# The next layer's norm moved into the last down product of a two-layer transformer block

## The chip, the cores and the metric

The kernel runs on one core of a Trainium2 chip. The metric is the device time of one execution in microseconds, inputs in HBM at the start and the output in HBM at the end. Engines: PE (TensorE) multiplies and transposes, ACT (ScalarE) squares, rounds and evicts, DVE (VectorE) does two-operand work, POOL (GpSimd) takes inverse roots and does part of the two-operand work, SP (SyncE) issues the DMAs.

## What is computed

Two layers of a block with 1024 tokens and model width 1024, all in float32:

```
for layer in range(2):
    h = rms_norm(x) * attn_norm[layer]
    d_q, d_k, d_v, m_cq, m_ckv, m_krope, r_q, r_k, r_v, r_g = split(h @ w_in[layer])
    mixed = concat(diff_attention(...), mla(...), retention(...))
    x = x + mixed @ w_out[layer]
    h = rms_norm(x) * ffn_norm[layer]
    x = x + (silu(h @ w_gate[layer]) * (h @ w_up[layer])) @ w_down[layer]
out = rms_norm(x) * final_norm
```

## The kernel before

Each float32 operand of a product is split into a high part that the fast matmul form holds exactly (ACT rounds it by a copy) and a low part, the difference (DVE or POOL subtracts). A product is three matmuls: high by high, high by low, low by high.

Every engine has its own program, and semaphores order them; there is no scheduler. The layer is a hardware loop on each engine (`with pe.Fori(0, DEPTH) as L` and its likes), so each wait on a count of `L * PER[name] + n` takes register instructions.

The 1024 tokens are 8 tiles of 128. `X` holds x as rows. The start of a layer is the norm: ACT squares the tiles in the order 4, 5, 6, 7, 0, 1, 2, 3 (`square_rows`), POOL takes the inverse roots of four tiles at a time (`inverse_roots`), DVE scales the four tiles into `rows` or `rows1` (`scale_rows`). PE then transposes each group of four tiles in 8 blocks of 4 transpositions (`transpose_rows`), one block to a PSUM bank, four banks in turn (`NORM_BANKS`). From a bank ACT writes the high part `ht_hi` (`high_rows`) and DVE the low part `ht_lo` (`low_rows`), and then the bank is free (`tr_free`). Tiles 4 to 7 go first, then 0 to 3; all 16 blocks come before the first projection. The weights of the first head (`w_diff` 0) are rounded by ACT in four quarters and their low parts are made by POOL (`weights(0)`).

Then comes differential attention, steps `a` from -8 to 33. Up to step -1 a step projects one tile (`diff_project`, unit `u = a + 8`, tile `7 - u`, 24 matmuls of 384 columns); from step -7 on the previous unit's q and k are transposed behind it (`diff_transpose`, 4 transpositions, banks 5 and 6 in turn, `TR_BANKS`, which `take_ring` hands out). ACT takes v from the projection (`diff_v`, tile `dv`), DVE and POOL rotate q and k, ACT and DVE write them into tiles that lie over `X`; so `X` is first stored to HBM (`x_saved`), and ACT waits for that.

The layer ends with the down product, 77 steps (`DN_STEPS`) of 12 matmuls of 512 columns, seven groups of 11. ACT and DVE prepare the operands of a step four to five steps ahead (`down_high`, `down_low`), and `take_down` adds a finished group's banks to `X`. Group 4, the sixth, completes tiles 4 to 7 of `X`. Group 3, the seventh, completes tiles 0 to 3 and uses banks 0 to 3; banks 4 to 7 are not written in it. SP's queue issues the load of the next operands, one DMA a step, then in the next pass of the loop eight small loads of parameters, the three loads of head 0's weights, the three of head 1's after the last down step, and the store of `X`.

## Time and profile before

| | |
|---|---|
| Time, median of 3 runs | 2698.19 us (2694.29 to 2698.67) |
| The profiled execution's own time | 2699.12 us |
| Its span, first to last instruction | 2697.2 us |
| Mean granted TensorE clock | 0.981 |
| PE busy | 2549.1 us, 95% of the span |
| DVE, ACT, POOL busy | 1532.3, 1095.3, 1015.7 us |
| Where the first layer's last matmul starts | 1344.07 us |

The rows further down are from this one execution. Its time is 1.9 us above its span and 0.93 us above the median. In a timeline row the first number is the start, the second the time from there to the end of the group, then engine, line, instruction, output and inputs, shape, and the count; in brackets stands how long the engine was idle before it and which instruction ended that.

### The profile page before, as it was taken

The numbers are of one execution on the slowest core, as the hardware profiler recorded it, in microseconds if no ns is written. First come the engines' busy times: TensorE is split into PE (matmuls) and PEld (weight loads), VectorE is DVE, ScalarE is ACT, GpSimd is POOL, SyncE is SP. The second block draws the span as 40 slices with busy tenths as digits, with TensorE's granted clock in tenths as the row PEclk, the third lists the DMA queues.
The fourth block names the chain that finished last, engine by engine and source line by source line (L and its number), as shares of the span: only waits on it lengthen the run. The fifth ranks groups of instructions, "written<-read, shape, count | busy, mean of one in ns | idle before, by whom it ended". The sixth has DMA issues, their size and how long they took to land. (4 is left out here: it accounts for less than half of the span.)

```text
span 2697.2 us, 43066 instructions
## 1 busy us (share of the span) xinstructions
PE 2549.1 (95%) x13054; PEld 2186.6 (81%) x13054; DVE 1532.3 (57%) x3045; ACT 1095.3 (41%) x2503; POOL 1015.7 (38%) x1161
## 2 busy tenths in 40 slices
PE   5999988999899999999989999989998999999997
PEld 5999877878688888888789998777786888888886
DVE  4666555382655454577656665444726544444885
ACT  4444554262522232344444545433625322232444
POOL 3455422173254545201044554221833454542012
PEclk9999999999999999999999999989999999999999
DMA  5111011023233333573321101011232333236633
GB/s 178 28 34 39 16 37 38 4 88 134 77 106 98 96 110 108 187 254 98 106 99 32 35 20 40 5 38 42 80 123 63 111 109 109 82 113 228 217 98 121
DMA packets 238651, 242.68 MB, mean 90 GB/s; under 512 B 27904, under 2 KB 171008, under 8 KB 238464
## 3 DMA queue, kind: packets, MB, share of 16 engines
q1 hardware_dynamic: 238464, 240.43, 27.8%
q8 instruction: 88, 1.44, 0.2%
q14 instruction: 99, 0.81, 0.1%
HBM read 172.75 MB, written 67.63 MB: 89 GB/s over the span
## 5 line engine op out<-in xcount | busy, mean ns | idle before, releaser
L2414 POOL TENSOR_TENSOR fw_a_lo<-fw_a_raw,fw_a_hi 128x512 fp32r<-128x512 f32 x132 | 179.7, 1362 | 468.0 <-DVE fw_s_raw L1996 468.0
L2414 POOL TENSOR_TENSOR fw_s_lo<-fw_s_raw,fw_s_hi 128x512 fp32r<-128x512 f32 x176 | 229.7, 1318 | 51.7 <-ACT fw_s_hi L1487 51.7
L723 PE MATMUL banks<-ht_hi,da_hi 128*128 128x512 f32 x496 | 192.9, 389 | 0.0
L723 PE MATMUL banks<-ht_lo,da_hi 128*128 128x512 f32 x496 | 192.9, 389 | 0.0
L723 PE MATMUL banks<-ht_hi,da_lo 128*128 128x512 f32 x496 | 192.9, 389 | 0.0
L723 PE MATMUL banks<-w_diff_hi,ht_hi 128*128 128x384 f32 x512 | 180.7, 353 | 6.3 <-DVE ht_lo L1674 4.3
L723 PE MATMUL banks<-w_diff_hi,ht_lo 128*128 128x384 f32 x512 | 172.8, 337 | 0.0
L723 PE MATMUL banks<-w_diff_lo,ht_hi 128*128 128x384 f32 x512 | 172.6, 337 | 0.0
L2241 POOL TENSOR_TENSOR qk_rot<-rope_a,rope_b 128x512 f32<-128x512 f32 x64 | 82.7, 1292 | 210.7 <-DVE rope_b L1703 210.7
L1731 DVE TENSOR_REDUCE stats<-banks 128x1 f32<-128x1024 f32 (+3 forms) x192 | 138.3, 748 | 32.8 <-PE banks L924 27.9
L723 PE MATMUL banks<-h_t_hi,fw_s_hi 128*128 128x512 f32 x352 | 139.8, 397 | 12.1 <-DVE h_t_lo L2000 8.2
L1561 ACT ACTIVATE u_two<-u_two 128x512 f32<-128x512 f32 x42 | 26.6, 632 | 284.0 <-DVE u_two L2107 284.0
L723 PE MATMUL banks<-h_t_hi,fw_s_lo 128*128 128x512 f32 x352 | 139.2, 395 | 0.0
L723 PE MATMUL banks<-h_t_lo,fw_s_hi 128*128 128x512 f32 x352 | 139.1, 395 | 0.0
L723 PE MATMUL banks<-ht_hi,fw_a_hi 128*128 128x512 f32 x352 | 137.4, 390 | 0.9 <-POOL fw_a_lo L2414 0.9
L723 PE MATMUL banks<-ht_hi,fw_s_hi 128*128 128x512 f32 x352 | 137.0, 389 | 0.0
L723 PE MATMUL banks<-ht_hi,fw_a_lo 128*128 128x512 f32 x352 | 137.0, 389 | 0.0
L723 PE MATMUL banks<-ht_hi,fw_s_lo 128*128 128x512 f32 x352 | 137.0, 389 | 0.0
L723 PE MATMUL banks<-ht_lo,fw_a_hi 128*128 128x512 f32 x352 | 137.0, 389 | 0.0
L723 PE MATMUL banks<-ht_lo,fw_s_hi 128*128 128x512 f32 x352 | 136.9, 389 | 0.0
L2064 DVE TENSOR_TENSOR da_lo<-da_raw,da_hi 128x512 fp32r<-128x512 f32 x154 | 117.1, 760 | 23.0 <-ACT da_hi L1538 23.0
L1299 ACT ACTIVATE pt_hi<-banks 128x512 fp32r<-128x512 f32 (+1 forms) x96 | 43.7, 490 | 205.1 <-PE banks L826 205.1
(357 smaller groups left out, 7497.7 us busy)
## 6 DMA issues: line engine op xcount, KB each, us to landing
da_raw<-act_scratch SPq DMA_DIRECT2D x154, 256.0 KB, 2.7
fw_a_raw<-in_w_gate_dram SPq DMA_DIRECT2D x88, 256.0 KB, 3.1
act_scratch<-act_s SPq DMA_DIRECT2D x66, 256.0 KB, 2.9
w_diff_raw<-in_w_in_dram SPq DMA_DIRECT2D x24, 512.0 KB, 6.0
fw_a<-in_w_up_dram SPq DMA_DIRECT2D x44, 256.0 KB, 3.2
fw_a_raw<-in_w_up_dram SPq DMA_DIRECT2D x44, 256.0 KB, 2.9
act_scratch<-act_zero SPq DMA_DIRECT2D x44, 256.0 KB, 2.4
act_scratch<-act_one SPq DMA_DIRECT2D x44, 256.0 KB, 2.8
```

Of the source, the lines that this page charges most:

```text
L723: mm = pe.matmul(bank, lhsT, rhs, start=first and i == 0, stop=last and i == len(pairs) - 1, skip_group_check=resumes)
L1299: act.activation(hi[:, b:b + n, :], banks[:, TR_BANKS[r % 2], 0:n * P].rearrange("p (b n) -> p b n", n=P), ACT.Copy).then_inc(S["tr_hi"], 1)
L1561: act.activation(u2[1 - m][:], u2[1 - m][:], ACT.Silu).then_inc(S["u_g1"], 1)
L1731: dve.tensor_reduce(neg_max[:, a % 2, m:m + 1], SCORE[j % 2][:, 0:(t + 1) * P], AX_X, ALU.max, negate=True)\
L2064: dve.tensor_tensor(a[1][:], a[2][:], a[0][:].bitcast(F32), ALU.subtract)
L2241: return pool.tensor_tensor(dst[:] if copies > 1 else dst[:].unsqueeze(2), a, b, ALU.add)
L2414: pool.tensor_tensor(w[1][:], w[2][:], w[0][:].bitcast(F32), ALU.subtract).then_inc(S["f_lo"], 1)
```

## The change

The layer loop becomes a Python loop on every engine, so the program of a layer is written out twice, and waits compare with constants. Within it three pieces move.

First, the norm of tiles 4 to 7 of the next layer (squares on ACT, `square_first`; scaling on DVE, `scale_first`; 32 transpositions on PE, `first_half`; high and low parts, `high_first`, `low_first`) is issued inside or right behind the last steps of the down product: the squares behind ACT's operands of the last four steps, the transpositions ahead of PE's last two steps. For the first layer they stand ahead of the layers.

Second, the 32 transpositions of tiles 0 to 3 (`second_half`) move behind the second and the third projection, 16 each, and use banks 5 and 6 of `take_ring` instead of four banks. In the second layer DVE scales those tiles at step -7, ahead of its rotation of the second unit.

Third, the low parts of head 0's weights go from POOL to DVE (`weights_first`, semaphore `w_lo0`); at the layer boundary DVE does them, ahead of `scale_first`. ACT rounds these weights behind its last square at the boundary, and behind the first half's high parts in the first layer. The store of `X` is split in two; the half with tiles 4 to 7 is issued ahead of head 1's loads. The exponentials of lambda move from the layer's start to step -4. The table load that ACT has before its first squares is gone from its program; one stands at step -4 of each layer instead, ahead of those exponentials.

```diff
+SECOND_HALF = {1 - T: range(KD // 2), 2 - T: range(KD // 2, KD)}
+SQUARE_STEP, TRANSPOSE_STEP = 4, 2
...
-            with sp.Fori(0, DEPTH) as L:
+            for L in range(DEPTH):
...
+                def save_x(half, done):
+                    tiles = slice(4 * half, 4 * half + 4)
+                    sp.wait_ge(S[f"x_in{half}"], 16)
+                    sp.wait_ge(S["x_done"], L * PER["x_done"] + done)
+                    arrives(x_dram.rearrange("(t p) d -> p t d", p=P)[:, tiles, :], X[:, tiles, :], f"x_saved{half}")
+
+                save_x(1, T // 2)
...
                 sp.wait_ge(S["d_step"], L * PER["d_step"] + STEP_CREDIT)
                 load_diff(1)
-
-                sp.wait_ge(S["x_in0"], 16)
-                sp.wait_ge(S["x_in1"], 16)
-                sp.wait_ge(S["x_done"], L * PER["x_done"] + X_CREDIT)
-                arrives(x_dram.rearrange("(t p) d -> p t d", p=P), X[:], "x_saved")
+                save_x(0, T)
 
...
+            def first_half(layer):
+
+                pe.wait_ge(S["n_xn"], layer * PER["n_xn"] + T // 2)
+                for k in range(KD):
+                    if k >= 4:
+                        pe.wait_ge(S["tr_free"], layer * PER["tr_free"] + k - 3)
+                    for j in range(4):
+                        tr = pe.transpose(banks[:, NORM_BANKS[k % 4], tokens(j)], rows[:, j, tokens(k)], ident[:])
+                    tr.then_inc(S["tr_done"], 1)
+
+            first_half(0)
+            for L in range(DEPTH):
+                ring, freed = [KD], [0]
 
...
-                transpose_rows(rows, "n_xn", 4)
-                transpose_rows(rows1, "n_xn", 8)
                 ring_empty()
 
+                def second_half(blocks):
+                    pe.wait_ge(S["n_xn"], L * PER["n_xn"] + T)
+                    for k in blocks:
+                        bank = take_ring()
+                        for j in range(4):
+                            tr = pe.transpose(bank[:, tokens(j)], rows1[:, j, tokens(k)], ident[:])
+                        tr.then_inc(S["tr_done"], 1)
 
...
+                    if a in SECOND_HALF:
+                        second_half(SECOND_HALF[a])
...
+                    if i == DN_STEPS - TRANSPOSE_STEP and L + 1 < DEPTH:
+                        first_half(L + 1)
...
+            def square_first(layer, i):
+
+                t = NORM_TILES[i]
+                if t % 4 == 0:
+                    act.wait_ge(S[f"x_in{t // 4}"], 16)
+                act.wait_ge(S["x_done"], layer * PER["x_done"] + i + 1)
+                if i:
+                    act.wait_ge(S["n_sq"], layer * PER["n_sq"] + i)
+                act.activation(row_square[:], X[:, t, :], ACT.Square, accum_out=row_ss[:, t:t + 1]).then_inc(S["n_sq"], 1)
+
+            def high_first(layer):
+                act.wait_ge(S["params_in"], layer * PER["params_in"] + PER["params_in"])
+                for k in range(KD):
+                    act.wait_ge(S["tr_done"], layer * PER["tr_done"] + k + 1)
+                    act.activation(ht_hi[:, k, tokens(4, 4)], banks[:, NORM_BANKS[k % 4], :], ACT.Copy,
+                                   scale=attn_gain[:, k:k + 1]).then_inc(S["tr_hi"], 1)
+
+            def weights_first(layer):
+                act.wait_ge(S["w_in0"], layer * PER["w_in0"] + 16 * 3)
+                for i in range(PARTS):
+                    k = slice(i * KD // PARTS, (i + 1) * KD // PARTS)
+                    act.activation(w_diff[0][0][:, k, :], w_diff[0][2][:, k, :], ACT.Copy).then_inc(S["w_hi"], 1)
+
+            for i in range(T):
+                square_first(0, i)
+            high_first(0)
+            weights_first(0)
+            for L in range(DEPTH):
+                ring = [KD]
...
-                for i, t in enumerate(NORM_TILES):
-                    if t % 4 == 0:
-                        act.wait_ge(S[f"x_in{t // 4}"], 16)
-                    square_rows(0, i, t, "x_done", i + 1)
-                act.wait_ge(S["params_in"], L * PER["params_in"] + PER["params_in"])
-                high_rows(1, attn_gain)
-                weights(0)
-                high_rows(0, attn_gain)
-
-                act.wait_ge(S["lam"], L * PER["lam"] + 2)
-                act.activation(lam_exp[:], lam_sum[:], ACT.Exp).then_inc(S["lam"], 1)
-
+                if L:
...
+                    if a in SECOND_HALF:
+                        high_second(SECOND_HALF[a])
+                    if a == 1 - T:
+                        act.wait_ge(S["x_saved0"], L * PER["x_saved0"] + 16)
...
+                    if L + 1 < DEPTH and i >= DN_STEPS - SQUARE_STEP:
+                        square_first(L + 1, i - DN_STEPS + SQUARE_STEP)
                     if i == PAIRS + B_RING - 1:
                         act.wait_ge(S["d_step"], L * PER["d_step"] + (PAIRS + STEP_CREDIT))
                         for j in range(4):
                             act.activation(d_s1[:, j, :], banks[:, j, :], ACT.Copy).then_inc(S["d_s1"], 1)
+                if L + 1 < DEPTH:
+                    weights_first(L + 1)
+                    act.wait_ge(S["db_lo"], L * PER["db_lo"] + PER["db_lo"])
+                    high_first(L + 1)
...
+            def weights_first(layer):
+                for i in range(PARTS):
+                    k = slice(i * KD // PARTS, (i + 1) * KD // PARTS)
+                    dve.wait_ge(S["w_hi"], layer * PER["w_hi"] + i + 1)
+                    w = dve.tensor_tensor(w_diff[0][1][:, k, :], w_diff[0][2][:, k, :], w_diff[0][0][:, k, :].bitcast(F32), ALU.subtract)
+                w.then_inc(S["w_lo0"], 1)
+
+            dve.wait_ge(S["params_in"], PER["params_in"])
+            scale_first(0, 1)
+            low_first(0, range(4))
+            scale_first(0, 0)
+            low_first(0, range(4, KD))
+            weights_first(0)
+            for L in range(DEPTH):
...
-                dve.wait_ge(S["params_in"], L * PER["params_in"] + PER["params_in"])
-                scale_rows(range(4, T), 1, (rows1, rows))
-
-                low_rows(1, attn_gain, range(4))
-                scale_rows(range(4), 2, (rows1, rows))
-                low_rows(1, attn_gain, range(4, KD))
-                low_rows(0, attn_gain)
-
                 for m in range(2):
...
+                    if L and a == 1 - T:
+                        scale_first(L, 0)
+                    if a == 5 - T:
+                        lambdas()
...
+                    if a in SECOND_HALF:
+                        low_second(SECOND_HALF[a])
...
+                if L + 1 < DEPTH:
+                    weights_first(L + 1)
+                    dve.wait_ge(S["params_in"], (L + 2) * PER["params_in"])
+                    scale_first(L + 1, 1)
+                    low_first(L + 1, range(KD))
                 take_down(3)
...
                 inverse_roots(0, [(4, T), (0, 4)], 0)
-                weights(0)
```

PE at the start of a layer, before: the last rows of the transpositions (`rows_225` is `rows1`, tiles 0 to 3) and what stands between them and the first projection (L723).

```order
L750 REGISTER_ALU
L744 REGISTER_ALU [waits n_xn]
L754 MATMUL banks<-ident,rows_225 128x128 [waits tr_free]
L754 MATMUL banks<-ident,rows_225 128x128 x3
...
L737 REGISTER_ALU
L760 ISA [waits tr_free]
L761 ISA [waits w_hi]
L723 MATMUL banks<-w_diff_hi,ht_hi 128x384 [waits w_lo]
L723 MATMUL banks<-w_diff_lo,ht_hi 128x384
```

PE in the first layer of the change, from the end of the second projection (L730) to the start of the third; `qk_rot_153` is the first unit's q and k.

```order
L730 MATMUL banks<-w_diff_hi,ht_lo 128x384
L804 MATMUL banks<-ident,rows_225 128x128 [waits n_xn]
L804 MATMUL banks<-ident,rows_225 128x128 x7
L804 MATMUL banks<-ident,rows_225 128x128 [waits tr_free]
L804 MATMUL banks<-ident,rows_225 128x128 x3
...
L819 MATMUL banks<-ident,qk_rot_153 128x128 [waits tr_free,rope_sum]
L819 MATMUL banks<-ident,qk_rot_153 128x128 x3
L730 MATMUL banks<-w_diff_hi,ht_hi 128x384 [waits z_free,w_lo0,w_hi]
```

The transpositions of tiles 0 to 3 no longer stand ahead of all projections, but behind two of them, and the third waits behind four blocks of them and the first unit's four transpositions.

PE in the change, in the last group of the first layer's down product: the last matmul of step 74, the transpositions of tiles 4 to 7 for the next layer, the first matmuls of step 75.

```order
L730 MATMUL banks<-db_hi_276,da_lo_268 128x512
L745 MATMUL banks<-ident,rows 128x128 [waits n_xn]
L745 MATMUL banks<-ident,rows 128x128 x15
L745 MATMUL banks<-ident,rows 128x128 [waits tr_free]
L745 MATMUL banks<-ident,rows 128x128 x3
...
L730 MATMUL banks<-ht_hi,da_hi_270 128x512 [waits db_lo]
L730 MATMUL banks<-ht_lo,da_hi_270 128x512
```

Steps 75 and 76 of the down product now stand behind a wait for `n_xn`, the count of tiles that DVE has scaled.

ACT at the layer boundary, before: the last operands of the down product (`da_hi`, then the other operand's high part) and the end of the hardware loop; the squares follow in the next pass.

```order
L1538 ACTIVATE da_hi_273<-da_raw_275 128x512 [waits da_in6]
L1551 REGISTER_ALU [waits wd22c]
L1553 ACTIVATE ht_hi<-wd_tail 128x512 [waits d_step]
L1211 REGISTER_ALU
L1211 COMPARE_AND_BRANCH
```

ACT there in the change: the last operands, the fourth square, the weights of head 0 (`w_diff_hi`), the high parts of tiles 4 to 7, the squares of tiles 0 to 3, and the first projection's v.

```order
L1599 ACTIVATE da_hi_273<-da_raw_275 128x512 [waits da_in6]
L1614 ACTIVATE ht_hi<-wd_tail 128x512 [waits d_step,wd22c]
L1249 ACTIVATE row_square,stats<-X 128x1024 [waits n_sq,x_done]
L1262 ACTIVATE w_diff_hi<-w_diff_raw 128x768 [waits w_in0]
L1262 ACTIVATE w_diff_hi<-w_diff_raw 128x768 x3
L1255 ACTIVATE ht_hi<-banks,stats 128x512 [waits tr_done,params_in,db_lo]
L1255 ACTIVATE ht_hi<-banks,stats 128x512 [waits tr_done] x7
L1249 ACTIVATE row_square,stats<-X 128x1024 [waits n_sq,x_done,x_in0]
L1249 ACTIVATE row_square,stats<-X 128x1024 [waits n_sq,x_done] x3
L1331 ACTIVATE dv_124<-banks 128x128 [waits z_done,x_saved1]
```

The high parts of tiles 4 to 7 and the weights have moved from behind all eight squares to behind four of them.

## Rows read from the trace of the kernel before

**Rows 1.** The page, engines: busy us (share of span) x instructions.
```profile
PE 2549.1 (95%) x13054; PEld 2186.6 (81%) x13054; DVE 1532.3 (57%) x3045; ACT 1095.3 (41%) x2503; POOL 1015.7 (38%) x1161
```

**Rows 2.** Waits of PE, whole span: us in total, times, longest.
```profile
PE banks L754 <- DVE rows L1662: 30.2, 4, 22.3
```

**Rows 3.** Timeline of PE, layer boundary: start, duration, instruction, count, idle before.
```profile
1344.07 0.39 PE L723 MATMUL banks<-ht_hi,da_lo 128*128 128x512 f32 x1
...
1351.89 5.70 PE L754 MATMUL banks<-ident,rows 128*128 128x128 f32 x32 [7.43 <-DVE rows L1662]
...
1360.25 5.82 PE L754 MATMUL banks<-ident,rows 128*128 128x128 f32 x32 [2.65 <-DVE ht_lo L1674]
...
1368.24 0.46 PE L723 MATMUL banks<-w_diff_hi,ht_hi 128*128 128x384 f32 x1 [2.18 <-DVE ht_lo L1674]
```

**Rows 4.** Timeline of ACT, second layer: a dv row starts when a projection ends.
```profile
1374.27 0.28 ACT L1277 ACTIVATE dv<-banks 128x128 fp32r<-128x128 f32 x1 [5.64 <-PE banks L723]
...
1378.43 0.28 ACT L1277 ACTIVATE dv<-banks 128x128 fp32r<-128x128 f32 x1 [3.88 <-PE banks L723]
...
1383.06 0.28 ACT L1277 ACTIVATE dv<-banks 128x128 fp32r<-128x128 f32 x1 [3.53 <-PE banks L723]
...
1387.66 0.28 ACT L1277 ACTIVATE dv<-banks 128x128 fp32r<-128x128 f32 x1 [3.51 <-PE banks L723]
```

**Rows 5.** Timeline of DVE, layer boundary.
```profile
1344.50 2.48 DVE L2172 TENSOR_TENSOR X<-X,banks 128x512 f32<-128x512 f32 x4 [12.24 <-PE banks L723]
...
1356.80 2.73 DVE L1662 TENSOR_SCALAR rows<-X,stats 128x1024 f32<-128x1024 f32 x4
...
1359.45 8.54 DVE L1674 SCALAR_TENSOR_TENSOR ht_lo<-banks,stats,ht_hi 128x512 fp32r<-128x512 f32 x12
```

**Rows 6.** Timeline of ACT, layer boundary.
```profile
1330.90 0.63 ACT L1553 ACTIVATE ht_hi<-wd_tail 128x512 fp32r<-128x512 f32 x1 [1.57 <-PE banks L723]
...
1345.30 1.06 ACT L1230 ACTIVATE row_square<-X 128x1024 f32<-128x1024 f32 x1 [5.37 <-DVE X L2172]
```

**Rows 7.** Timeline of POOL, layer boundary: the second root.
```profile
1350.64 1.40 POOL L2199 TENSOR_TENSOR stats<-stats 128x4 f32<-128x4 f32 x1
```

**Rows 8.** Timeline of SP's queue, layer boundary.
```profile
1290.09 35.69 SPq L516 DMA_DIRECT2D da_raw<-act_scratch  x14
...
1329.30 0.39 SPq L516 DMA_DIRECT2D stats<-in_attn_norm_dram  x1
...
1333.59 14.01 SPq L516 DMA_DIRECT2D w_diff_raw<-in_w_in_dram  x6
```

**Rows 9.** DMA issues at 1333 to 1344: KB each, us to landing.
```profile
w_diff_raw<-in_w_in_dram SPq DMA_DIRECT2D x3, 512.0 KB, 7.2
```

**Rows 10.** DMA issues at 1344 to 1350: KB each, us to landing.
```profile
x_scratch<-X SPq DMA_DIRECT2D x1, 4096.0 KB, 15.5
```

**Rows 11.** Timeline of all engines, first layer's start.
```profile
11.89 1.28 ACT L1230 ACT_TABLE_LOAD   x1
...
22.30 6.02 PE L754 MATMUL banks<-ident,rows 128*128 128x128 f32 x32 [22.30 <-DVE rows L1662]
...
29.22 3.05 ACT L1224 ACTIVATE w_diff_hi<-w_diff_raw 128x768 fp32r<-128x768 f32 x4
...
30.05 8.43 DVE L1674 SCALAR_TENSOR_TENSOR ht_lo<-banks,stats,ht_hi 128x512 fp32r<-128x512 f32 x12
...
38.70 0.43 PE L723 MATMUL banks<-w_diff_hi,ht_hi 128*128 128x384 f32 x1 [2.15 <-DVE ht_lo L1674]
```

**Rows 12.** Timeline of ACT, first layer: the fourth projection's end.
```profile
56.54 0.28 ACT L1277 ACTIVATE dv<-banks 128x128 fp32r<-128x128 f32 x1 [3.51 <-PE banks L723]
```

**Rows 13.** Windows: length, busy of PE, PEld, DVE, ACT, POOL, then granted clock.
```profile
80.00:88.00 8.00, 6.30 (x33) 5.37 (x33) 5.96 (x10) 2.61 (x5) 1.27 (x1) 1.00 0.28 67
...
1412.00:1420.00 8.00, 6.30 (x25) 5.39 (x24) 6.66 (x10) 2.34 (x4) 1.27 (x1) 0.79 0.16 38
...
1368.00:1372.00 4.00, 3.76 (x13) 3.76 (x14) 0.87 (x7) 0.20 (x1) 0.00 (x0) 0.57 0.02 6
```

More of the change, by code:

```diff
@@ L87 @@
 DIFF_STEPS = range(-T, DIFF_HEADS * T + 2)
+SECOND_HALF = {1 - T: range(KD // 2), 2 - T: range(KD // 2, KD)}
+SQUARE_STEP, TRANSPOSE_STEP = 4, 2
 def diff_rings():
-    ring, after = 2 * KD, {}
+    ring, after = KD, {}
     for a in DIFF_STEPS:
+        ring += len(SECOND_HALF.get(a, ()))
         if 0 <= a - 1 < DIFF_HEADS * T:
@@ L1647, in _, with scale_first, low_first @@
             dve.wait_ge(S["tab_act"], 1)
-            with dve.Fori(0, DEPTH) as L:
-                ring, high = [0], [0]
+            def scale_first(layer, half):
+                dve.wait_ge(S["n_rstd"], layer * PER["n_rstd"] + (1 if half else 2))
+                for j in range(4):
+                    t = 4 * half + j
+                    dve.tensor_scalar((rows if half else rows1)[:, j, :], X[:, t, :], row_rstd[:, t:t + 1], None, ALU.mult)\
+                        .then_inc(S["n_xn"], 1)
+            def low_first(layer, blocks):
+                for k in blocks:
+                    dve.wait_ge(S["tr_hi"], layer * PER["tr_hi"] + k + 1)
+                    at_ = tokens(4, 4)
+                    dve.scalar_tensor_tensor(ht_lo[:, k, at_], banks[:, NORM_BANKS[k % 4], :], attn_gain[:, k:k + 1],
+                                             ht_hi[:, k, at_].bitcast(F32), ALU.mult, ALU.subtract).then_inc(S["tr_free"], 1)
+            def weights_first(layer):
[11 more added lines that the diff above has]
+            for L in range(DEPTH):
+                ring, high = [KD], [KD]
                 def low_ring():
@@ L2199, in inverse_root @@
                 return pool.tensor_tensor(out_, in_, minus_half[:, 0:in_.shape[1]], ALU.pow)
-            with pool.Fori(0, DEPTH) as L:
+            for L in range(DEPTH):
                 def inverse_roots(norm, groups, done):
```

52 lines of the change are left out of this document (34 added, 18 removed).

## Prediction

> **What bounds the kernel now.** I read the page first: PE is busy for 95% of the span [rows 1], so a microsecond counts only if it adds or removes idle time of PE, work of PE, or a stretch at its lower clock. PE's waits put the norm's share at 30.2 us in four places, of which 22.3 us are the time before the first transposition of all [rows 2]. Then I read PE's timeline at the boundary between the layers. The last matmul of the down product starts at 1344.07, and the first projection at 1368.24. Between lie 7.43 us of waiting for squares, root and scaling, 5.70 us of transpositions, 2.65 us of waiting, 5.82 us of transpositions, 2.18 us of waiting [rows 3]. That projection then ends at 1374.27 and the next one 4.16 us later [rows 4]; the first took 6.0 us, since the granted clock was 0.57 in its first 4 us [rows 13], the lower of the two levels (1.2 GHz) for most of it: about 1.7 us lost. The fourth projection, my mark in both layers, ends at 1387.66 in the second layer [rows 4] and at 56.54 in the first [rows 12].
>
> **What a moved transposition costs.** Before, 32 transpositions take 5.7 to 5.8 us with four banks, partly at the low clock [rows 3]; PE stands idle around them anyway. In the change the 32 of tiles 0 to 3 come behind the second and third projection, where PE has no idle time: successive projection ends are 4.16 us apart without transpositions, 4.63 and 4.60 with four (1378.43, 1383.06, 1387.66) [rows 4], so four transpositions cost 0.46 us of a busy PE. A piece of 16 costs 1.85 us if nothing waits. But they have two banks now. A bank comes free when ACT has copied it (0.69 us, my estimate; a copy of 128x512 between SBUF tiles takes 0.63 [rows 6]) and DVE has subtracted (8.54 us for 12 gives 0.71 us each [rows 5]). From a projection's end I count: block 0 and 1 written at 0.5 and 1.0; ACT on block 0 to 1.2, DVE to 1.95; block 2 written at 2.65 (with 0.2 us of signal and drain), ACT to 3.35, DVE to 4.1; then the q and k transpositions, which take block 2's bank, to 4.75. Without the change they would end at 0.46. So a piece adds 4.3 us, the two pieces 8.6 us a layer. The bound below is 3.7 us a layer (no waits), the bound above 8.6 plus clock losses.
>
> **First layer.** The first squares lose the table load ahead of them, 1.28 us [rows 11]; I count it in full. PE's first transpositions (22.30, 6.02 us long) are thus at 21.0 to 27.0. DVE's low parts start the second time at 30.05, twelve in 8.43 us, 0.70 apart [rows 11]; only four remain ahead of the weights, to 32.9, less 1.28 is 31.6. The weights' low parts are new on DVE: four of 128x768. The nearest rows are four two-operand adds of 128x512 in 2.48 us [rows 5], 0.62 each; times 1.5 is 0.93, with overlap 3.6 us for four (bounds 3.4 and 3.8). ACT has rounded the first quarter long before (29.22 plus 0.8, less 1.28 [rows 11]). First projection: 35.3, against 38.70 before [rows 11]. PE has then been idle for 8 us, longer than the 7.43 us after which the boundary shows the low clock, so I give it the 6.0 us of the second layer's first projection: ends 41.3, then 45.5. Then piece (4.75), projection (4.16), piece, projection: 63.3. Before: 56.54. **The first layer loses 6.8 us.**
>
> **The boundary.** A down step takes 2.72 us: 14 loads, one a step, in 35.69 us [rows 8]. Step 75, of 0 to 76, would start at 1344.46 less 5.44, at 1339.0. PE waits there until DVE has scaled tiles 4 to 7, and DVE does the weights first. The squares fit: ACT stands idle 1.57 us in a step [rows 6] and a square takes 1.06 [rows 6] plus a short readout; they end at about 1333. The weights decide. SP's last operand load is issued by 1325.78, the small loads begin only at 1329.30 and the weights' at 1333.59 [rows 8]; the 3.5 us between are the end of the loop, as nothing is waited for. Unrolled, the weights' load starts at 1330.1. Before, the third lands some 7.7 us after the first issue (7.2 us median from issue [rows 9]); so they are there at 1337.8. ACT's first quarter takes 0.8, DVE 3.6, scaling 2.73 [rows 5]: PE goes on at 1345.1, **6.1 us late**. Queued behind it are two steps of the down product, and behind these `take_down(3)`, the last squares and all that follows. The transpositions take 5.7 us as they did before [rows 3] (four banks, the same copies behind them), the two steps 5.44: the product ends at 1356.2, against 1344.46. High and low parts of tiles 4 to 7 are finished by then and hidden. Two projections at the full clock end at 1364.6. Meanwhile `take_down(3)`, squares and root follow the product's end as before: the root ends at 1350.64 plus 1.40, 7.6 us after it [rows 7], here 1363.8; scaling to 1366.5. PE waits 1.9 us once more. Piece, projection, piece, projection: 1384.4, against 1387.66. **The boundary gains 3.3 us.**
>
> SP: the second half of the store is issued behind head 1's loads. The whole store of 4 MB took 15.5 us from issue [rows 10]; half of it, issued at about 1359.5 behind 1.5 MB, lands around 1369 to 1370 by my estimate. ACT waits for it ahead of the first q and k at about 1371, so it costs nothing, with 1 to 2 us of cover; each further microsecond of delay would hold the third projection. POOL only loses work. ACT's new table load at step -4 is hidden: it is idle for 3.5 us in a projection step [rows 4].
>
> **Registers.** Counting the programs' rows, a layer of PE loses some 700 register instructions, ACT and DVE as many. Where an engine is busy they lie behind its work. They can only lengthen a wait that is passed while another stands behind it. The view of waits has some 100 waits of PE in the whole span; at 0.015 us each (a choice near the 0.04 us of a whole hop, below) that is 1.5 us. The bounds are 0 and 10 us (0.1 each).
>
> **Sum.** Plus 6.8, minus 3.3, minus 1.5 is plus 2.0 us. The pieces leave PE idle for some 2 of 5 us, four times. Two stretches of 8 us, one in each layer and both with 6.30 us of PE work, differ: one has clock 1.00, the other 0.79 [rows 13]. At 1.7 us a fall I add one of four: plus 3.7 us on 2699.12. The profiled execution is 0.93 us above the median, so against the median's kind of run: **2702 us**. A difference under 0.2%, 5.4 us, is about what cannot be told from none.
>
> **Rivals.**
> - *Forecast: the pieces on two banks eat what the boundary gives.* 2702, own range 2697 to 2708. Chance 0.45.
> - *Faster: the register instructions count on every hop.* In latency-bound stretches a result passes ACT, DVE and POOL before PE gets it. If each of the 100 waits of PE is 0.1 us shorter, 10 us go: 2693. It decides above 0.12 us a wait, given the plus of 5 us from the rest. For it: there are many such instructions. Against: the one hop that the rows show, from PE's last matmul (ends 1344.46) to DVE's add at 1344.50 [rows 3, 5], takes 0.04 us with registers in the program. Chance 0.16.
> - *The clock falls in each piece.* Four falls instead of one: plus 5 us, 2707; with a fall in the last down steps too, 2709. For it: the second stretch of [rows 13]. Against: the first one, with the same idle time. Chance 0.19.
> - *The weights land later at the boundary,* since the store of tiles 4 to 7 (2 MB) is issued right behind them and shares the DMA engines, or SP gains nothing from the unrolled loop: 3.5 us later, 2705.5; with the store's other half late too, 2709. Chance 0.12.
> - *PE does not wait at step 75,* because the weights are early: 6 us less, 2696. Against: [rows 8, 9] would have to be off by 6 us. Chance 0.08.
>
> The Trainium skill, page "TensorE: Matmul & The Clock Gate", section "A second HAM failure mode: psum-queue depth-cycling", describes a kernel that cycles through PSUM banks, idles briefly between groups of matmuls, and so loses and regains its clock again and again. By that rule the third case would hold, 2707 instead of 2702. The trace has it both ways [rows 13], and I keep to one fall.
>
> **How the numbers follow.** Slower by over 0.2% (above 2703.6): a third of the forecast's 0.45, nearly all of the clock's 0.19, most of the late weights' 0.12: 0.42. Faster (below 2692.8): half of the register case and tails of the others: 0.14. Within: 0.44. The range, 2692 to 2710, leaves out the far half of the register case and the worst of the clock and weights cases.
>
> **What would show it.** In the changed kernel: first projection at 35 in the first layer, fourth ending near 63; a wait of PE for `rows` of 6 us near 1352 (all is 7 us later there) inside the down product; 1.9 us more before the second layer's first piece; ACT and DVE alternating in each piece with PE idle twice for about 1 us; the distance from the first layer's fourth projection to step 75 shorter by what the registers cost. I am wrong if the pieces cost under 3 us each, if PE hardly waits at step 75, or if the long middle stretches of the layers become shorter by more than 5 us.

## The result, and the profile after

The changed kernel takes 2713.97 us (median of 11 executions, 2708.59 to 2739.28); the kernel before took 2698.43 beside it (11 executions). The ratio is 1.0071, with an interval of 1.0057 to 1.0085: **slower**, by 15.5 us between the medians (a ratio of 1.0058), 12 us above the prediction of 2702 and 4 us above the top of its range. The first ratio is the larger one because two long executions, of 2736.30 and 2739.28 us, weigh in it: the means of all 11 have a ratio of 1.0072, and of 1.0056 without these two. Of the 22 executions of the kernel before beside the variants in the last four rows of the table below, one took 9174.9 us, and the ratios leave it out. The executions whose traces are compared here took 2711.45 and 2699.12 us, so 12.3 us are to be explained.

The page of the changed kernel, span and engines (busy us, share, instructions):

```profile
span 2709.6 us, 38529 instructions
...
PE 2550.3 (94%) x13054; PEld 2189.5 (81%) x13054; DVE 1547.5 (57%) x3053; ACT 1096.4 (40%) x2503; POOL 1000.0 (37%) x1153
```

PE has the same number of instructions and 1 us more of busy time than in [rows 1]. That is a balance: in the two rebuilt places (first and third part of the table below) PE is busy 5.2 us longer and idle 8.5 us longer, and in the last part it is busy 4.2 us less. The view of PE's waits, changed kernel (us in total, times, longest), shows which kinds are new:

```profile
PE banks L745 <- DVE rows L1720: 29.0, 2, 22.2
...
PE banks L730 <- DVE w_diff_lo L1734: 7.9, 1, 7.9
...
PE banks L804 <- DVE ht_lo L1790: 4.5, 4, 1.1
...
PE banks L819 <- DVE ht_lo L1790: 3.8, 4, 1.0
...
PE banks L804 <- DVE rows L1720: 2.7, 1, 2.7
```

Against [rows 2] the longest wait is as long as it was (22.2 and 22.3 us: the first transposition of all), though a table load was taken away ahead of it. The eight waits of about 1 us each are the two in each of the four pieces.

Three marks cut the kernel into parts: the fourth projection's end in each layer (a `dv` row of ACT) and the end of step 74 of the first layer's down product. Timeline of ACT, changed kernel, the first four projections of each layer:

```profile
42.93 0.28 ACT L1331 ACTIVATE dv<-banks 128x128 fp32r<-128x128 f32 x1 [10.61 <-PE banks L730]
...
47.03 0.28 ACT L1331 ACTIVATE dv<-banks 128x128 fp32r<-128x128 f32 x1 [3.83 <-PE banks L730]
...
57.68 0.28 ACT L1331 ACTIVATE dv<-banks 128x128 fp32r<-128x128 f32 x1 [4.51 <-PE banks L730]
...
68.15 0.28 ACT L1331 ACTIVATE dv<-banks 128x128 fp32r<-128x128 f32 x1 [4.41 <-PE banks L730]
...
1375.47 0.26 ACT L1331 ACTIVATE dv<-banks 128x128 fp32r<-128x128 f32 x1
...
1378.26 0.28 ACT L1331 ACTIVATE dv<-banks 128x128 fp32r<-128x128 f32 x1 [2.53 <-PE banks L730]
...
1392.26 0.28 ACT L1331 ACTIVATE dv<-banks 128x128 fp32r<-128x128 f32 x1 [4.52 <-PE banks L730]
...
1402.72 0.28 ACT L1331 ACTIVATE dv<-banks 128x128 fp32r<-128x128 f32 x1 [4.40 <-PE banks L730]
```

These answer to [rows 4] and [rows 12]. Timeline of PE, changed kernel: the norm of tiles 4 to 7 inside the down product, and the first piece of the second layer (answers to [rows 3]):

```profile
1358.68 5.73 PE L745 MATMUL banks<-ident,rows 128*128 128x128 f32 x32 [6.77 <-DVE rows L1720]
...
1380.90 1.09 PE L804 MATMUL banks<-ident,rows 128*128 128x128 f32 x8 [2.67 <-DVE rows L1720]
1383.12 1.97 PE L804 MATMUL banks<-ident,rows 128*128 128x128 f32 x8 [1.13 <-DVE ht_lo L1790]
1385.89 1.09 PE L819 MATMUL banks<-ident,qk_rot 128*128 128x128 f32 x4 [0.80 <-DVE ht_lo L1790]
```

Step 74 ends at 1358.68 less 6.77, 1351.91; before it was 1339.02 (the product's end at 1344.46 less two steps, 5.44). The parts:

| part | before | changed | difference | forecast |
|---|---|---|---|---|
| start to the fourth projection, layer 1 | 56.54 | 68.15 | +11.6 | +6.8 |
| from there to the end of step 74 | 1282.48 | 1283.76 | +1.3 | registers, -1.5 in the whole span |
| from there to the fourth projection, layer 2 | 48.64 | 50.81 | +2.2 | -3.3 |
| from there to the end of the span | 1309.54 | 1306.88 | -2.7 | |
| span | 2697.2 | 2709.6 | +12.4 | |

The forecast counted one clock fall of 1.7 us somewhere in these. Both places that the change rebuilt came out worse than forecast, by 4.8 and 5.5 us.

### The profile page after: what moved, and what is told of

It reads as the page before. It is cut to its first block, busy times and chain, and to the rows that moved or that the text cites. A ratio compares the mean times of both kernels' runs of the same rounds, so it can differ in the third digit from the quotient of the medians.

```text
span 2709.6 us, 38529 instructions
## 1 busy us (share of the span) xinstructions
PE 2550.3 (94%) x13054; PEld 2189.5 (81%) x13054; DVE 1547.5 (57%) x3053; ACT 1096.4 (40%) x2503; POOL 1000.0 (37%) x1153
## 4 chain that ended last, share of the span: by engine, by line
PE 85%; DVE 6%; POOL 3%; ACT 3%; issue 2%; SPq 1%; DMA 1%; POOLq 0%; DVEq 0%; ACTq 0%
PE banks L730 76%; PE banks L852 2%; PE banks L844 2%; PE banks L819 1%; DVE stats L1826 1%; PE banks L971 1%; SPq L519 1%; PE banks L845 1%; POOL stats L2305 1%; PE banks L772 1%; DVE mpt L1851 0%; POOL r_at_lo L2460 0%; DVE rows L1720 0%; PE banks L1000 0%; PE banks L934 0%
## 5 line engine op out<-in xcount | busy, mean ns | idle before, releaser
L730 PE MATMUL banks<-ht_hi,da_hi 128*128 128x512 f32 x496 | 193.0, 389 | 0.0
L730 PE MATMUL banks<-ht_hi,da_lo 128*128 128x512 f32 x496 | 193.0, 389 | 0.0
L730 PE MATMUL banks<-ht_lo,da_hi 128*128 128x512 f32 x496 | 192.9, 389 | 0.0
L730 PE MATMUL banks<-w_diff_hi,ht_hi 128*128 128x384 f32 x512 | 182.6, 357 | 10.3 <-DVE w_diff_lo L1734 7.9
L730 PE MATMUL banks<-w_diff_hi,ht_lo 128*128 128x384 f32 x512 | 174.1, 340 | 0.0
L730 PE MATMUL banks<-w_diff_lo,ht_hi 128*128 128x384 f32 x512 | 174.1, 340 | 0.0
L730 PE MATMUL banks<-h_t_hi,fw_s_hi 128*128 128x512 f32 x352 | 139.6, 396 | 12.1 <-DVE h_t_lo L2101 8.1
L730 PE MATMUL banks<-h_t_lo,fw_s_hi 128*128 128x512 f32 x352 | 138.9, 395 | 0.0
L730 PE MATMUL banks<-h_t_hi,fw_s_lo 128*128 128x512 f32 x352 | 138.8, 394 | 0.0
L730 PE MATMUL banks<-ht_hi,fw_a_hi 128*128 128x512 f32 x352 | 137.4, 390 | 0.9 <-POOL fw_a_lo L2519 0.9
L730 PE MATMUL banks<-ht_lo,fw_a_hi 128*128 128x512 f32 x352 | 137.0, 389 | 0.0
L730 PE MATMUL banks<-ht_hi,fw_s_hi 128*128 128x512 f32 x352 | 137.0, 389 | 0.0
L730 PE MATMUL banks<-ht_hi,fw_a_lo 128*128 128x512 f32 x352 | 137.0, 389 | 0.0
L730 PE MATMUL banks<-ht_hi,fw_s_lo 128*128 128x512 f32 x352 | 136.9, 389 | 0.0
L730 PE MATMUL banks<-ht_lo,fw_s_hi 128*128 128x512 f32 x352 | 136.9, 389 | 0.0
```

Source lines behind the costliest of these rows:

```text
L730: mm = pe.matmul(bank, lhsT, rhs, start=first and i == 0, stop=last and i == len(pairs) - 1, skip_group_check=resumes)
```

## The experiments

Times are medians of all executions; ratios are to the kernel before, run beside it on the same chip. "Mark 1" is the fourth projection's end in the first layer; "boundary" is the distance from the end of step 74 to the fourth projection of the second layer. These two are from one execution of each kernel.

| kernel | us | ratio, interval | mark 1 | boundary |
|---|---|---|---|---|
| before | 2698.43 | | 56.54 | 48.64 |
| changed | 2713.97 | 1.0071, 1.0057 to 1.0085 | 68.15 | 50.81 |
| layers unrolled alone | 2696.46 | 0.9995, 0.9983 to 1.0007 | 57.72 | 44.47 |
| changed, own banks | 2694.82 | 0.9991, 0.9982 to 1.0001 | 58.74 | 41.89 |
| changed, tiles ahead of weights | 2706.23 | 1.0026, 1.0017 to 1.0036 | 68.57 | 43.53 |
| changed, both of these | 2687.27 | 0.9952, 0.9935 to 0.997 | 58.27 | 34.17 |
| changed, idle time filled | 2707.05 | 1.0032, 1.002 to 1.0044 | 64.54 | 48.35 |
| changed, parameters later | 2710.96 | 1.0055, 1.0033 to 1.0078 | 65.49 | 50.65 |
| changed, tiles 0 to 3 scaled last | 2710.82 | 1.0063, 1.0036 to 1.0091 | 64.10 | 51.13 |
| all four edits of order and banks | 2684.59 | 0.9947, 0.9934 to 0.996 | 56.23 | 34.20 |

**Layers unrolled alone.** The kernel before, with nothing but this, on each of the five engines:

```diff
-            with pe.Fori(0, DEPTH) as L:
+            for L in range(DEPTH):
```

> Only one part of the change: the kernel before with the layer loop written out on all five engines, no instruction moved. Theory P (the loss comes from the four pieces of 16 transpositions behind the projections: their waits for two banks and the falls of the clock after them): the same time as before, 2698 us (2694 to 2702). Rival U (the doubled program itself costs, through code loading or other timing of waits): 2705 us or more. The forecast's term for register instructions (1.5 us less, bounds 0 to 10): 2697.

The ratio holds 1: the register instructions are worth neither the 10 us of the faster rival nor anything else that this measurement can tell (the interval reaches from 4.6 us less to 1.9 us more). Nor does a program written out twice cost anything that the times show. The whole loss is in the moved work.

The boundary is another matter: here it takes 44.47 us, 4.2 less than before. Timeline of DVE at the boundary: the first scaling in the kernel before (its `take_down(3)` is the first row of [rows 5]), then `take_down(3)` and the first scaling with the layers unrolled alone:

```profile
1349.09 2.74 DVE L1662 TENSOR_SCALAR rows<-X,stats 128x1024 f32<-128x1024 f32 x4 [2.12 <-issue]
```

```profile
1350.48 2.48 DVE L2172 TENSOR_TENSOR X<-X,banks 128x512 f32<-128x512 f32 x4 [12.18 <-PE banks L723]
1352.88 2.73 DVE L1662 TENSOR_SCALAR rows<-X,stats 128x1024 f32<-128x1024 f32 x4
```

At the end of the hardware loop DVE stands idle for 2.12 us with nothing that it waits for; written out, it goes on at once, and PE's wait for the scaled tiles is 5.22 us where it was 7.43. Another 1.5 us is the clock: the first projection of the second layer takes 4.53 us (1371.61 to 1376.14) and not 6.03. In the first layer it is the other way round (6.09 and 4.46), and the part between the marks is 4.8 us longer here, so that the total shows no gain. Each of these is one execution.

**Own banks.** Banks 0 to 3 are idle while a layer starts. The transpositions of tiles 0 to 3 take them in turn, and the first two units' q and k take banks 5 and 6 without waiting, so PE waits for no copy in a piece:

```diff
                     for k in blocks:
-                        bank = take_ring()
+                        if k >= 4:
+                            pe.wait_ge(S["tr_free"], L * PER["tr_free"] + second_ring[k - 4])
+                        ring[0] += 1
+                        second_ring[k] = ring[0]
+                        bank = banks[:, k % 4, :]
...
-                    bank = take_ring()
+                    if u < 2:
+                        bank = banks[:, TR_BANKS[ring[0] % 2], :]
+                        ring[0] += 1
+                    else:
+                        bank = take_ring()
```

ACT's and DVE's copies read `banks[:, k % 4, :]` accordingly.

> The changed kernel, but the transpositions of tiles 0 to 3 go to the four banks 0 to 3, which nothing uses before step 0, so that PE never waits for a bank inside a piece. Theory P: each piece with its q and k transpositions falls from 5.2 to 5.7 us to about 2.4, and the projection behind it from 5.4 to 5.6 us to 4.2, since the clock does not fall: four times some 4 us, 16 us in all, 2698 us. Were only the waits the cost and not the clock: 11 us less, 2703. Rival U or S (the wait at step 75 is the loss): at most 4 us less, 2710 or more.

19 us came back, more than the 16 expected: the kernel is now level with the one before. By the rows the four steps with a piece take 25.5 us together where they took 42.7, which is 17.2 of it; in the execution compared, the first projection also ended 1.0 us earlier, which the edit does not touch. Timeline of PE, own banks, both pieces of the first layer:

```profile
45.83 1.91 PE L810 MATMUL banks<-ident,rows 128*128 128x128 f32 x16
47.57 0.60 PE L829 MATMUL banks<-ident,qk_rot 128*128 128x128 f32 x4
...
52.19 1.91 PE L810 MATMUL banks<-ident,rows 128*128 128x128 f32 x16
53.93 0.60 PE L829 MATMUL banks<-ident,qk_rot 128*128 128x128 f32 x4
```

and of the changed kernel, the same place:

```profile
46.84 1.04 PE L804 MATMUL banks<-ident,rows 128*128 128x128 f32 x8
...
49.01 1.31 PE L804 MATMUL banks<-ident,rows 128*128 128x128 f32 x8 [1.14 <-DVE ht_lo L1790]
...
51.32 1.09 PE L819 MATMUL banks<-ident,qk_rot 128*128 128x128 f32 x4 [1.00 <-DVE ht_lo L1790]
...
57.48 1.04 PE L804 MATMUL banks<-ident,rows 128*128 128x128 f32 x8
...
67.96 0.60 PE L819 MATMUL banks<-ident,qk_rot 128*128 128x128 f32 x4
```

From the start of one piece to the start of the next, a piece and a projection take 52.19 less 45.83, 6.36 us, without waits and 57.48 less 46.84, 10.64 us, with them. The waits that the rows name, two of 1.1 and 1.0 us, are only part of the 4.3 us between.

**Idle time filled.** Is the rest the clock? Here the waits stay, but seven transpositions whose result nothing reads stand ahead of each of them:

```diff
                         tr.then_inc(S["tr_done"], 1)
+                        if k % 2:
+                            for j in range(7):
+                                pe.transpose(banks[:, 3, tokens(j % 4)], rows1[:, j % 4, tokens(k)], ident[:])
```

> The changed kernel with work added: in each of the four pieces that stand ahead of a projection, seven transpositions whose result nothing reads are issued into the idle bank 3 ahead of the two places where TensorE waits for a ring bank (1.0 to 1.1 us each). The waits keep their place, but TensorE is busy in them. Theory C (of the 19 us that taking the ring waits away gave back, a good part was the clock: it falls to half behind a piece with two idle stretches): the pieces keep their 5.2 us, the projection behind each runs at 0.17 us a matmul from its start and takes 4.2 us and not 5.4 to 5.6, so 4 times 1.3 us, about 5 us less than the changed kernel: 2709. Theory W (only the waits cost time, and the clock would fall anyway): 2714, with the projections behind still at 5.4 to 5.6 us. A third outcome: the filling work itself ends behind the waits and lengthens the pieces, each by some tenths of a us: up to 2716.

Work was added and the kernel became 6.9 us faster than the changed one by the medians, where 5 were expected; the intervals of the two ratios do not meet, and without the changed kernel's two long executions its ratio of means, 1.0056, still lies above the interval here. Timeline of PE, idle time filled, first layer:

```profile
46.09 1.04 PE L804 MATMUL banks<-ident,rows 128*128 128x128 f32 x8
46.96 0.93 PE L808 MATMUL banks<-ident,rows 128*128 128x128 f32 x7
48.26 1.31 PE L804 MATMUL banks<-ident,rows 128*128 128x128 f32 x8 [0.38 <-DVE ht_lo L1793]
49.42 0.93 PE L808 MATMUL banks<-ident,rows 128*128 128x128 f32 x7
50.58 0.63 PE L822 MATMUL banks<-ident,qk_rot 128*128 128x128 f32 x4 [0.23 <-DVE ht_lo L1793]
...
55.22 1.04 PE L804 MATMUL banks<-ident,rows 128*128 128x128 f32 x8
```

The step with a piece takes 55.22 less 46.09, 9.13 us, against 10.64, with the waits in the same places. What changed is the granted clock. Windows of the changed kernel (length, busy us of PE, PEld, DVE, ACT, POOL, then the clock):

```profile
46.00:50.00 4.00, 2.86 (x21) 2.35 (x20) 2.27 (x5) 1.84 (x4) 1.27 (x1) 1.00 0.00 0
50.00:54.00 4.00, 3.00 (x13) 2.79 (x12) 2.20 (x4) 1.71 (x4) 0.00 (x0) 0.65 0.01 2
```

and with the idle time filled:

```profile
46.00:50.00 4.00, 3.62 (x31) 3.11 (x30) 2.59 (x6) 2.58 (x5) 1.27 (x1) 1.00 0.00 0
50.00:54.00 4.00, 3.77 (x26) 3.56 (x23) 1.94 (x4) 0.96 (x3) 0.00 (x0) 1.00 0.02 4
```

After the piece with idle stretches the clock falls to the lower of its two levels (1.2 GHz) for part of the projection behind it (0.65 in the mean of that window); after the filled piece it stays at the upper one (2.4 GHz). A fall costs 10.64 less 9.13, 1.5 us. In the second layer the projections behind both filled pieces have a clock of 1.00 too, but the first of these pieces, which stands behind a wait of 2.67 us, still runs in part at the lower level (0.50 from 1382 to 1384 us), and its step takes 9.70 us. The four steps take 37.1 us against 42.7 in the changed kernel's execution above, and against 40.0 to 41.4 in the three below, so they account for 3 to 6 of the 6.9 us. So a piece costs, over a step with four q and k transpositions (4.61 us, [rows 4]): 1.75 us of work, 2.8 us of waiting (9.13 less 6.36), and 1.5 us of clock where it falls.

**The changed kernel three times more.** Not edited.

> The changed kernel once more, one look: some of its executions (2 of 11) took 2736 to 2739 us at a granted clock of 0.967 where the others took 2709 to 2717 at 0.977. Theory C (the idle stretches in a piece leave the clock low for longer in such an execution): if this look catches one, its windows show one stretch of some tens of us behind a piece at half clock. Rival: the clock is lower somewhere that has nothing to do with the pieces. If it catches none, its rows repeat those of the changed kernel, with the granted clock at 0.55 to 0.65 behind each of the four pieces.

> As the look before it: the changed kernel once more, to catch one of its executions at 2736 to 2739 us and to see where in it the granted clock is lower, behind a piece (theory C) or elsewhere (rival). If it is an execution at 2709 to 2717 us, its clock falls to 0.55 to 0.65 behind each of the four pieces, as in the first profile.

> As the two looks before it, a third time: about one execution in five is of the longer kind by the runs so far. Behind a piece (theory C) or elsewhere (rival); else a repetition of the four falls of the clock.

They took 2709.08, 2708.44 and 2708.82 us (the kernel before 2695.61 beside them), so none was of the long kind and neither account of it could be tested. The other expectation, a fall behind each of the four pieces, did not hold. In the four executions of this kernel that have a trace, the steps with a piece took, in us:

| execution | first layer | second layer |
|---|---|---|
| first | 10.6, 10.5 | 11.2, 10.5 |
| second | 9.1, 10.7 | 11.1, 9.1 |
| third | 9.1, 10.7 | 11.0, 9.1 |
| fourth | 10.6, 9.1 | 11.2, 10.5 |

At 9.1 us the clock stayed up. So the same four pieces give four, two, two and three falls; the second layer's first piece, which stands behind a wait of 2.7 us, gives one each time. The three variants that keep the two banks and are not filled (tiles ahead of weights, parameters later, tiles 0 to 3 scaled last) have falls in 10 of 12 steps, so there are 21 in 28 in all; the three variants with own banks have none in 12 (6.35 to 6.41 us each, though the second layer's first piece stands behind a wait of 2.4 to 2.7 us there too). The last of the four executions, first layer:

```profile
46.53 1.03 PE L804 MATMUL banks<-ident,rows 128*128 128x128 f32 x8
...
57.13 1.03 PE L804 MATMUL banks<-ident,rows 128*128 128x128 f32 x8
...
66.25 0.60 PE L819 MATMUL banks<-ident,qk_rot 128*128 128x128 f32 x4
```

10.60 us from the first of these rows to the second, 9.12 from the second to the third, with the same waits in both.

**Tiles ahead of weights.** At the boundary DVE and ACT prepare the first head's weights ahead of the tiles, and PE waits 6.77 us for the scaled tiles in the middle of the down product. Here both do the tiles first:

```diff
                 if L + 1 < DEPTH:
-                    weights_first(L + 1)
                     dve.wait_ge(S["params_in"], (L + 2) * PER["params_in"])
                     scale_first(L + 1, 1)
                     low_first(L + 1, range(KD))
+                    weights_first(L + 1)
```

and on ACT `weights_first(L + 1)` goes behind `high_first(L + 1)`.

> The changed kernel, but at the layer boundary DVE scales tiles 4 to 7 and makes their low parts ahead of the low parts of the weights, and ACT makes their high parts ahead of the weights. Theory S (the wait of 6.8 us at step 75 is caused by the weights ahead in DVE's queue): the wait goes, step 75 starts some 6 to 7 us earlier, 2707 us. New risk: the weights' low parts are then ready only about when the first projection wants them, up to 2 us of wait there, 2709. Rival: the wait has another cause (root or squares late): no change, 2714.

7.7 us came back, to 2706.2 where 2707 was expected. Timeline of PE, this kernel: the wait at step 75 is gone, and the 32 transpositions take 4.9 us with a short wait in them where they took 5.73:

```profile
1356.04 1.91 PE L745 MATMUL banks<-ident,rows 128*128 128x128 f32 x16
1358.29 2.63 PE L745 MATMUL banks<-ident,rows 128*128 128x128 f32 x16 [0.34 <-DVE ht_lo L1727]
```

Nothing took its place, which was the rival: the weights' low part is ready at 1366.3, when the product ends, and the first projection starts at 1366.46. Timeline of DVE, this kernel:

```profile
1351.41 2.74 DVE L1720 TENSOR_SCALAR rows<-X,stats 128x1024 f32<-128x1024 f32 x4 [1.92 <-POOL stats L2305]
...
1362.76 3.55 DVE L1734 TENSOR_TENSOR w_diff_lo<-w_diff_raw,w_diff_hi 128x768 fp32r<-128x768 f32 x4
```

**Both.** Own banks and tiles ahead of weights together.

> Both edits of the two kernels before this one together. If theory P and theory S both hold, the gains add: 16 and 7 us less than the changed kernel, 2691 us, some 7 us faster than the kernel before. If the pieces' cost only hid behind the wait or the reverse, less than the sum: 2695 to 2699.

2687.27 us: 26.7 less than the changed kernel, where the two alone gave 19.2 and 7.7. They add up (2691 was expected, from smaller single gains), and the kernel beats the one before by 0.5%. The boundary takes 34.17 us against 48.64 before. Of these 14.5 us, 4.2 are there with the layers unrolled alone (44.47); the moved norm is worth the other 10.3, once nothing waits in its new places but for tiles 0 to 3 (2.36 us ahead of the first piece).

**Parameters later.** The taken-away table load brought nothing, as DVE waits for the small parameters (they land at 19.4 us) ahead of the first scaling, which doesn't read them. Edit in the changed kernel:

```diff
-            dve.wait_ge(S["params_in"], PER["params_in"])
             scale_first(0, 1)
+            dve.wait_ge(S["params_in"], PER["params_in"])
```

> The changed kernel with one wait moved: in front of the first layer VectorE scales tiles 4 to 7 before, not after, it waits for the small parameters of the norm (the scaling doesn't read them). In the changed kernel's trace the scaling starts at 19.43 us while the root is there at 18.4. Theory P (that wait is what swallowed the gain of the table load that was taken away): the scaling starts at 18.4, and the first projection, and the kernel, are 1.0 us earlier: 2713. Rival: the parameters' arrival gates the next step too (the high and low parts read the gain), or the weights' high part does: no gain, 2714.

The rows of DVE show it. Changed kernel, then this one:

```profile
19.43 2.74 DVE L1720 TENSOR_SCALAR rows<-X,stats 128x1024 f32<-128x1024 f32 x4 [9.06 <-DMA stats<-in_ffn_norm_dram]
...
27.33 2.73 DVE L1720 TENSOR_SCALAR rows<-X,stats 128x1024 f32<-128x1024 f32 x4
29.98 2.72 DVE L1727 SCALAR_TENSOR_TENSOR ht_lo<-banks,stats,ht_hi 128x512 fp32r<-128x512 f32 x4
32.61 3.55 DVE L1734 TENSOR_TENSOR w_diff_lo<-w_diff_raw,w_diff_hi 128x768 fp32r<-128x768 f32 x4
```

```profile
18.56 2.74 DVE L1720 TENSOR_SCALAR rows<-X,stats 128x1024 f32<-128x1024 f32 x4 [8.14 <-POOL stats L2305]
```

The scaling starts 0.87 us earlier, and the first projection too (35.44 against 36.31). The median, 3 us lower, can't confirm so small a step: its interval overlaps that of the changed kernel.

**Tiles 0 to 3 scaled last.** In the first layer, `scale_first(0, 0)` behind `low_first(0, range(4, KD))` and `weights_first(0)` on DVE.

> The changed kernel with one step moved: in front of the first layer VectorE scales tiles 0 to 3 (4 operations of 0.68 us, 2.7 us) behind the low parts of tiles 4 to 7 and of the first weights, and not ahead of them. Theory S (this scaling is on the path to the first projection, which waits 7.9 us for the weights' low part): the first projection starts at 33.6 and not 36.3 us, and the kernel is 2.7 us shorter: 2711.3. Rival: VectorE waits for the high part of the weights on ScalarE anyway, and nothing or only a part comes back: 2713 to 2714.

By the rows it works as expected. Timeline of PE in this kernel, then in the changed one, the first projection:

```profile
33.90 0.66 PE L730 MATMUL banks<-w_diff_hi,ht_hi 128*128 128x384 f32 x1 [5.51 <-DVE w_diff_lo L1734]
```

```profile
36.31 0.66 PE L730 MATMUL banks<-w_diff_hi,ht_hi 128*128 128x384 f32 x1 [7.93 <-DVE w_diff_lo L1734]
```

2.4 us earlier. The median (2710.82) is 3.2 us lower than the changed kernel's, but three of its 12 executions were of the long kind and the intervals overlap, so the times alone don't settle it.

**All four edits.**

> The kernel with both earlier edits (transpositions of tiles 0 to 3 into banks of their own without waits, and VectorE's and ScalarE's steps for tiles 4 to 7 ahead of those for the weights at the layers' boundary), which took 2687.3 us, and with the two edits of the first layer above it (parameters waited for behind the scaling, tiles 0 to 3 scaled last). If the two add: 2687.3 less 1.0 less 2.7, 2683.6 us. Rival: the first projection needs the weights' high part, which ScalarE makes behind its high parts of the tiles, so that less comes back: 2685 to 2687.

2684.59 us, ratio 0.9947. Against the kernel with two edits that is 2.7 us less, where 3.7 were expected; the intervals overlap. The rows have the first projection at 33.18 against 35.61, 2.4 us: the parameters had landed earlier in the other kernel's execution (18.90), so that edit had only 0.3 us to give beside it.

## Why the prediction was wrong

The mechanisms were the forecast ones: pieces that wait for two banks, a wait at step 75, falls of the clock. The number of falls was taken too small, and so were several smaller terms in both rebuilt places, so that the boundary lost where a gain was forecast. The forecast was plus 3.7 us and the traces show plus 12.4. Of the 8.7 between, the falls are 4.3 (four of 1.5 us, where one of 1.7 was counted) and the smaller terms below the rest.

- **The step that failed: "the pieces leave PE idle for some 2 of 5 us, four times ... I add one [fall] of four".** In the trace against which it was made there was one stretch with the clock at 1.00 and one at 0.79 [rows 13], and I chose the kinder, with a chance of 0.19 for a fall in each piece. The pieces gave two to four falls of 1.5 us in four executions (four in the one compared), and filling the idle time took 6.9 us off the median. The rival "the clock falls in each piece" came closest, but at 2707 it was low by 7 us too, as it kept the other terms. The stretches of [rows 13] are other steps, with other waits; they say that a fall can come, not how often it comes in another pattern of work. With two or three falls instead of four, as in the three later executions, this term would have been short by 1.3 to 2.8 us only; the count in the execution compared is partly luck. The Trainium skill, page "TensorE: Matmul & The Clock Gate", section "A second HAM failure mode: psum-queue depth-cycling", describes a kernel that cycles through PSUM banks and whose clock goes down and up because TensorE idles briefly between groups of matmuls. The runs agree with it in kind (21 falls in 28 steps with waits, none in 12 without), but here a piece now and then keeps its clock.
- **"A piece of 16 adds 4.3 us."** Without a fall it adds 9.13 less 4.61, 4.5 us. Right, and its make-up (work 1.75, waiting 2.8) too.
- **First layer, "loses 6.8 us": 11.6.** The missing 4.8 are: the first projection starts at 36.31 and not 35.3 (1.0), as the table load's 1.28 us, "counted in full", was shadowed by the wait for the parameters, which in the kernel before hid behind it; it takes 6.6 and not 6.0 us (0.6); the two steps with a piece take 10.65 and 10.47 and not 8.91 us (3.3, of which 3.0 are two falls). The same projections' start shows that the added weight work on DVE was sized well: 3.55 us against 3.6.
- **Boundary, "gains 3.3 us": loses 2.2.** "6.1 us late at step 75" was 6.77 (the weights' load is issued at 1342.66, and ACT's rounding starts 8.9 us later, when they are there, where 7.7 was counted; ACT and DVE then take 7.2 us, as forecast, though the prediction's own terms add up to 1344.9 and not 1345.1), the product ends 0.8 us later than forecast relative to step 74. The wait of 1.9 before the first piece was 2.67: DVE scales tiles 0 to 3 in 3.76 us where it took 2.73 [rows 5]. Then the two steps took 11.33 and 10.46 and not 8.91 us: 4.0 us, the largest part, with two falls in it (3.0).
- **Registers, -1.5:** unrolling alone made no difference that can be told in the whole (ratio 0.9983 to 1.0007); the view of PE's waits counts 88 of them in the kernel before, not some 100, and what the loop does cost at the boundary is the 2.12 us of DVE, a term that the prediction has only for SP. The first middle stretch (+1.3) says nothing: in four executions of the changed kernel it took 1283.8, 1284.7, 1288.2 and 1285.0 us. The last one (-2.7) may be real: it took 1309.5 us before and 1309.3 with the layers unrolled alone, but 1302.8 to 1307.5 in all eleven traces of the changed kernel and its variants. What gives these microseconds back no run here shows.

The first of DVE's four scalings of tiles 0 to 3 in the second layer, with its neighbour on POOL:

```profile
1377.08 1.78 DVE L1720 TENSOR_SCALAR rows<-X,stats 128x1024 f32<-128x1024 f32 x1 [0.36 <-POOL stats L2305]
```

```profile
1377.02 1.29 POOL L2346 TENSOR_TENSOR qk_rot<-rope_a,rope_b 128x512 f32<-128x512 f32 x1
```

This first scaling takes 1.78 us and lies beside the POOL operation of 1.29 us; the other three, with POOL idle, take 2.0 us together, as usual. The store of `X` is not the cause: the DMA engines were fully busy (share 0.99 to 1.05) beside all four, and also (1.02) beside the scaling before, which took 2.73. The other ten traces of the changed kernel and its variants have the same 3.76 or 3.77 us. That POOL causes it is still argued from the overlap; no run took it away.

Where the gain went, then: unrolling and the moved norm are worth 14.5 us at the boundary (4.2 and 10.3), and the first layer could be had at no loss (mark 1 at 56.23 with all edits, 56.54 before). Against this, 11 us went to waits for two PSUM banks in the pieces (4 times 2.8), 3 to 6 to the clock behind them, 7 to one misplaced preparation on DVE, 2.4 to another in the first layer.

## What to carry to other kernels

Work that is moved out of an idle stretch into a busy one keeps its own waits: a piece of 16 transpositions cost 2.8 us of waiting on a ring of two banks and none on four idle banks; so look for buffers that are free at the new place before the ring that is used there is shared. Price such a piece at three terms, work, waiting and the clock, and when the trace shows the clock both ways, count the fall for most pieces rather than for one (here 21 of 28). When a step is taken off the path, name the wait that was hidden under it (here the parameters' load), and when one is put into another engine's queue, put first what the busy engine needs first. When a change has several parts, measure each part's share where it acts: 4.2 of the boundary's 14.5 us came with the unrolled loop.

## What was not expected of the hardware

- Adding 56 transpositions that nothing reads, 14 in each of the four pieces, made the kernel 6.9 us faster; the granted clock of the projections behind them stayed at 1.00.
- At the end of the hardware loop DVE stood idle for 2.12 us, on the path to the first scaling, with nothing to wait for; with the layers written out the gap is gone.
- The clock's fall is not steady: the same piece, with the same waits to within 0.01 us, was followed by 9.1 us in some executions and by 10.6 in others.
- The changed kernel and the two variants of its first layer had executions of 2734.7 to 2740.2 us with a mean granted clock of 0.966 to 0.968, 6 of 36, where the others had 0.976 to 0.984. None of the 49 executions of the other six variants did so. None fell into a profile, so where the clock is lost in them stays open.
